# A DiT layer on one Trainium2 core: block-wise storage, one-piece streams and 64-byte gaps for the first feed-forward block's activations

## The reference

```python
mx = split(silu(c) @ ada_w + ada_b, 9)           # shift, scale, gate, three times; mc the same from c_ctx
x = x + 0.5 * mx[2] * swiglu(modulate(rmsnorm(x, norm_ffn1), mx[0], mx[1]), ffn1_w1, ffn1_w3, ffn1_w2)
y = y + 0.5 * mc[2] * swiglu(modulate(rmsnorm(y, norm_ffn1), mc[0], mc[1]), ffn1_w1, ffn1_w3, ffn1_w2)
...
# context keys and states, HGRN2 and Hyena groups of x, w_out
...
x = x + 0.5 * mx[8] * swiglu(modulate(rmsnorm(x, norm_ffn2), mx[6], mx[7]), ffn2_w1, ffn2_w3, ffn2_w2)
return rmsnorm(x, final_norm)
```

## Time and profile before

| | us |
|---|---|
| median of 3 runs | 3288.76 |
| the runs | 3288.66, 3288.76, 3296.98 |
| the profiled execution, its own time | 3298.05 |
| its span, first to last instruction | 3294.4 |
| TensorE busy in the span | 3176.7 (96%) |
| first feed-forward block, first to last matmul | about 228 to 1720 |
| second feed-forward block | about 2520 to 3280 |

### The profile page before, as it was taken

The page is one execution under the profiler, slowest core; times in us unless marked ns, Lnnn a source line. Parts: engine busy times, 40 slices in busy tenths (PEclk is TensorE's granted clock), DMA queues, the critical chain, the costliest instruction groups (busy, mean ns, idle before and its releaser), DMA issues.

```text
span 3294.4 us, 49838 instructions
## 1 busy us (share of the span) xinstructions
PE 3176.7 (96%) x19388; PEld 2796.4 (85%) x19388; DVE 2035.0 (62%) x2657; ACT 1183.0 (36%) x1538; POOL 132.5 (4%) x173
## 2 busy tenths in 40 slices
PE   6979999999999999999988899999998999999998
PEld 2338888888888888888878899999998999999998
DVE  5558747558465675665456567776666555555556
ACT  3122121222222222222236677763334443344434
POOL 1000000000000000000000013430000000000000
PEclk8989999999999999999998999999999999999999
DMA  7647544535446676665323454546544665655563
GB/s 255 224 168 209 168 148 147 179 128 177 150 130 217 204 248 219 220 201 167 99 83 117 139 162 150 154 134 199 165 143 148 183 185 181 184 180 183 179 184 128
DMA packets 438914, 563.28 MB, mean 171 GB/s; under 512 B 17855, under 2 KB 395064, under 8 KB 437896
## 3 DMA queue, kind: packets, MB, share of 16 engines
q1 hardware_dynamic: 432208, 545.80, 52.7%
q0 software_dynamic: 2816, 9.43, 0.9%
q10 hardware_dynamic: 3768, 6.37, 0.6%
HBM read 553.14 MB, written 8.39 MB: 170 GB/s over the span
## 4 chain that ended last, share of the span: by engine, by line
PE 89%; DVE 5%; ACT 2%; issue 2%; DMA 1%; SPq 0%; ACTq 0%; DVEq 0%
PE bank L415 27%; PE bank L416 27%; PE bank L417 27%; PE bank L1070 2%; PE bank L1123 1%; PE bank L649 1%; ACT w_hi L400 1%; PE bank L1311 1%; PE bank L1322 1%; DVE xn L471 1%; PE bank L1230 1%; DMA ada_over<-in_ada_w_dram 1%; DVE csum L958 1%; DVE w_lo L405 1%; PE bank L1111 1%
## 5 line engine op out<-in xcount | busy, mean ns | idle before, releaser
L405 DVE TENSOR_TENSOR w_lo<-raw,w_hi 128x1024 fp32r<-128x1024 f32 x736 | 911.6, 1241 | 963.1 <-ACT w_hi L400 958.8
L400 ACT ACTIVATE w_hi<-raw 128x1024 fp32r<-128x1024 f32 x736 | 774.7, 1057 | 1434.3 <-PE bank L417 1423.2
L415 PE MATMUL bank<-h_hi,w_hi 128*128 128x512 f32 (+1 forms) x2816 | 953.1, 338 | 23.3 <-DVE h_lo L483 20.0
L417 PE MATMUL bank<-h_hi,w_lo 128*128 128x512 f32 (+1 forms) x2816 | 951.1, 338 | 0.0
L416 PE MATMUL bank<-h_lo,w_hi 128*128 128x512 f32 (+1 forms) x2816 | 951.1, 338 | 0.0
L415 PEld LDWEIGHTS bank<-h_hi,w_hi 128*128 128x128 f32 x2816 | 538.2, 191 | 80.5 <-issue 15.8
L416 PEld LDWEIGHTS bank<-h_lo,w_hi 128*128 128x128 f32 x2816 | 538.3, 191 | 55.4
L417 PEld LDWEIGHTS bank<-h_hi,w_lo 128*128 128x128 f32 x2816 | 537.9, 191 | 55.7
L415 PE MATMUL bank<-g_hi,w_hi 128*128 128x512 f32 (+1 forms) x1408 | 476.1, 338 | 5.4 <-DVE g_lo L789 4.7
L416 PE MATMUL bank<-g_lo,w_hi 128*128 128x512 f32 (+1 forms) x1408 | 475.2, 337 | 0.0
L417 PE MATMUL bank<-g_hi,w_lo 128*128 128x512 f32 (+1 forms) x1408 | 474.9, 337 | 0.0
(11 more groups left out here) (244 smaller groups left out, 2796.0 us busy)
## 6 DMA issues: line engine op xcount, KB each, us to landing
raw<-in_ffn_w_dram SPq DMA_DIRECT2D x528, 512.0 KB, 3.6
ada_raw<-in_ada_w_dram SPq DMA_DIRECT2D x260, 512.0 KB, 4.5
raw<-in_w_in_dram SPq DMA_DIRECT2D x176, 512.0 KB, 3.8
raw<-in_w_out_dram SPq DMA_DIRECT2D x32, 512.0 KB, 3.6
ada_over<-in_ada_w_dram SPq DMA_DIRECT2D x28, 512.0 KB, 4.6
spec<-spec_spill POOLq DMA_DIRECT2D x8, 768.0 KB, 5.1
spec_spill<-spec_out ACTq DMA_DIRECT2D x4, 1280.0 KB, 5.1
xin<-in_x_dram SPq DMA_DIRECT2D x1, 2048.0 KB, 9.2
```

The lines of the kernel that those rows point to most:

```text
L400: nc.scalar.activation(w_hi[un.slot(j)][:], raw[un.slot(j)][:], ACT.Copy).then_inc(hi_done, 1)
L405: nc.vector.tensor_tensor(w_lo[un.slot(j)][:], raw[un.slot(j)][:], w_hi[un.slot(j)][:].bitcast(F32), ALU.subtract).then_inc(lo_done, 1)
L415: nc.tensor.matmul(o, w_hi[slot][:, c0:c0 + P], hi, start=start, stop=False, skip_group_check=True)
L417: return nc.tensor.matmul(o, w_lo[slot][:, c0:c0 + P], hi, start=False, stop=stop, skip_group_check=True)
```

## The change

`h1_hi` and `h1_lo` become 16 tiles each, one for each block `kb`, `[P, 2, SEQ]`: the 256 latent and the 256 context columns of a block lie side by side, 2 KB in one piece. The matmul's moving pattern becomes (512 at a step of 1). Behind each of the 32 tiles lies a tile of 16 numbers (64 bytes) that nothing reads or writes, so the tiles start 2112 bytes apart, at offsets 128, 192, 256, ... past a multiple of 1024. The gaps take 2048 bytes of a partition. The same amount is freed by declaring `rows` in the scope `first`, which closes before the feed-forward tiles are declared; `rows` now lies between `window` and `fw1`, and its room is part of the room of the `h1` tiles. All tiles from `cols` to `window`, and those of the later stages, lie 2048 bytes lower; `raw`, `w_hi`, `w_lo`, `x_res`, `g1_hi` and `g1_lo` lie where they were. No instruction is added, removed or moved on any engine, and no wait is added: matmuls, activations and vector operations have the same order, the same sizes and the same counters. Only addresses and that one access pattern differ.

```diff
--- before.py
+++ after.py
@@ -33,6 +33,7 @@
 N_CHUNK = FF // CHUNK
 N_MOD = 9
 EPS = 1e-6
+GAP = 16
 HEADS = 8
 PAIRS = HEADS // 2
 DK = 128
@@ -173,7 +174,6 @@
         ones_d = sb("ones_d", [P, P])
         ones_h = sb("ones_h", [P, P])
         ones_1 = sb("ones_1", [P, P])
-        rows = [sb(f"rows{n}", [P, P]) for n in range(4)]
         cols = [sb(f"cols{n}", [P, P]) for n in range(4)]
         mods = sb("mods", [P, N_MOD, KB, 2])
         silu_c = sb("silu_c", [P, KB, 2])
@@ -206,6 +206,7 @@
         dft = sb("dft", [P, T_COLS], scope=first)
         emb = sb("emb", [FILT_EMB, SEQ], scope=first)
         window = sb("window", [P, TB, HY], scope=first)
+        rows = [sb(f"rows{n}", [P, P], scope=first) for n in range(4)]
         fw1 = sb("fw1", [FILT_EMB, FILT_ORDER], scope=first)
         fw23 = sb("fw23", [FILT_ORDER, 2, FILT_ORDER], scope=first)
         fbias = sb("fbias", [FILT_ORDER, 4], scope=first)
@@ -229,8 +230,15 @@
         ada_wide = ada_raw + ada_over
         first.close()
         ffn = ExitStack()
-        h1_hi = sb("h1_hi", [P, 2, KB, SEQ], F32R, scope=ffn)
-        h1_lo = sb("h1_lo", [P, 2, KB, SEQ], F32R, scope=ffn)
+        h1_hi, h1_lo = [], []
+        for kb in range(KB):
+            letter = "abcdefghijklmnop"[kb]
+            h1_hi.append(sb(f"h1_hi_{letter}", [P, 2, SEQ], F32R, scope=ffn))
+            sb(f"h1_hi_gap_{letter}", [P, GAP], scope=ffn)
+        for kb in range(KB):
+            letter = "abcdefghijklmnop"[kb]
+            h1_lo.append(sb(f"h1_lo_{letter}", [P, 2, SEQ], F32R, scope=ffn))
+            sb(f"h1_lo_gap_{letter}", [P, GAP], scope=ffn)
         g1_hi = [sb(f"g1_hi{b}", [P, 512], F32R, scope=ffn) for b in range(FBLK)]
         g1_lo = [sb(f"g1_lo{b}", [P, 512], F32R, scope=ffn) for b in range(FBLK)]
         ffn.close()
@@ -499,7 +507,7 @@
 
             return vectors[:, bass.ds(kb, 1), t:t + 1].rearrange("p a c -> p (a c)")
 
-        n1["hi_ap"] = lambda t, kb: h1_hi[:, t, kb, :]
+        n1["hi_ap"] = lambda t, kb: h1_hi[kb][:, t, :]
         nctx["hi_ap"] = lambda t, kb: hc_hi[:, kb, :]
         n2["hi_ap"] = lambda t, kb: h2_hi[:, kb, :]
 
@@ -1160,7 +1168,7 @@
             to_columns(ADA_BEFORE - 1)
 
             pe.wait_ge(fs_out, 20)
-            ffn_pe(pe, fa, U_FFN1, lambda k: h1_hi[:, :, k, :], lambda k: h1_lo[:, :, k, :], g1_hi, g1_lo, 512, F1_LOOPS,
+            ffn_pe(pe, fa, U_FFN1, lambda k: h1_hi[k][:], lambda k: h1_lo[k][:], g1_hi, g1_lo, 512, F1_LOOPS,
                    n1["lo"])
 
             norm_pe(pe, nctx, 512)
@@ -1787,10 +1795,10 @@
             ve.wait_ge(mod_done, 3)
             ve.wait_ge(fs_spec, 20)
             ve.wait_ge(fs_dma, 32 * 4)
-            modulate_dve(ve, n1, 0, [x_res, y_res], lambda t, kb: h1_lo[:, t, kb, :], (0, 1), 0, 2, 0, 8)
+            modulate_dve(ve, n1, 0, [x_res, y_res], lambda t, kb: h1_lo[kb][:, t, :], (0, 1), 0, 2, 0, 8)
             take(ADA_BEFORE - 1)
             ve.wait_ge(mod_done, 6)
-            modulate_dve(ve, n1, 0, [x_res, y_res], lambda t, kb: h1_lo[:, t, kb, :], (0, 1), 0, 2, 8, KB)
+            modulate_dve(ve, n1, 0, [x_res, y_res], lambda t, kb: h1_lo[kb][:, t, :], (0, 1), 0, 2, 8, KB)
             ffn_dve(ve, fa, U_FFN1, g1, g1_hi, g1_lo, 512, [x_res, y_res], 0, F1_LOOPS, nctx)
 
             ve.wait_ge(ada_out, 1 + 2 * N_MOD)
```

## The result

| | before | after |
|---|---|---|
| median | 3291.80 us (6 runs, 3288.66 to 3296.98) | 3314.89 us (6 runs, 3312.88 to 3318.94) |
| ratio | | 1.0068, 95% interval 1.0058 to 1.0078 |
| profiled execution | 3298.05 us | 3312.88 us |

What follows compares the result with a forecast made beforehand. TensorE, busy 96% of the span, was taken as the bound. All terms were 0, so 3298.05 us stayed 3298; the forecast was the median level, 3288.8 us, ranging from 6 us under the lowest runs to 3299 us.

Steps and rivals of the forecast that it cites:

- What bounds the kernel: Whole kernel: TensorE busy for 96% of the span, so a change counts by matmul distance or what TensorE waits for.
- One piece in place of two: 4224 matmuls over `h`, first feed-forward block: reading 512 columns in one run instead of two changes nothing, 0 us.
- Gaps of 64 bytes: The 32 `h` tiles start at offsets stepping by 64 bytes: taken as 0; far end 13.4 ns more per matmul.
- The nearest rows: Prologue float32 matmuls of 512 columns, starting at offsets 128 and 960: both median 592 ns, read as no offset cost.
- the 2.3 ns at which the prediction said it would fail: Distance of two starts over `h`, forecast 226.6 ns: the forecast fails if it moves by more than 2.3 ns.
- an odd offset costs something: Slower rival, matmuls over `h`: 30 of 32 tiles cost 13.4 ns more per matmul, 53 us, to 3342 us; chance 4%.
- The rival in which the common offset makes up the fixed part: Faster rival, matmuls over `h`: two runs or shared offset cause the 13.4 ns; up to 56.6 us less, 3232 us; 5%.
- the fixed part: 13.4 ns before each `fp32r` matmul whatever its size, worked out from 226.6 ns at 512 columns and 120.0 at 256.
- The writes, the row tiles, the 2048 bytes: ScalarE and VectorE writes of `h` halves, `rows` freed with the prologue, other tiles moved by 2048 bytes: 0 each.
- Low-clock stretches: Slower rival, pauses between loops of the first feed-forward block: more stretches of 1.6 to 3.2 us; 3299 to 3302; 3%.
- the five stretches of the earlier trace: First feed-forward block, profiled execution: five short stretches at granted clock 0.54 to 0.72, said to cost 11.2 us.
- the two levels: Times of whole runs: the median's level, 3288.8 us, and an upper level, about 3297 to 3298 us.

Runs made afterwards that it cites:

- the kernel with the row tiles alone: The kernel before with only the row tiles freed with the prologue and an unused 2048-byte tile behind `h1_lo`: 3293.12 us, ratio 1.0000.

## Why the prediction was wrong, step by step

- **What bounds the kernel.** Right: TensorE's distance of starts set the time, and nearly all of the change lies in it.
- **One piece in place of two: 0.** Right. One piece without gaps gave 226.7 ns and a ratio of 0.9989; the rule of the Trainium skill that was weighed there ("Advanced Engine Details and Errata", section "PSUM Cachelines") did not show for the moving operand; its section is on PSUM, and neither kernel changes the pattern that the matmuls write.
- **Gaps of 64 bytes: 0.** Wrong, and this is the step that failed. The nearest rows, plain float32 matmuls at offsets of 128 and 960, follow each other only every 428 ns or so, and their durations were taken as proof for a stream of half that distance. The prediction named that weakness and took the value anyway. The rows also compared absolute offsets, which the kernel with everything 64 bytes further showed to play no part. What counts is the distance to the weights, and the prediction did not read these rows for it: by the order of the declarations `dft`, the weights of `tsum` and `tdif`, starts where `h1_hi` does, so those two stood 64 bytes past their weights all along, and at their slow pace no cost showed. The prediction also had no row of an `fp32r` stream at another offset, and treated that absence as a small matter; the absence was the whole question, for the kernel before had every such stream at the offset of its weights. The measured price is 5.1 ns x 4224 = 21.5 us, 226.8 to 231.9 ns, over twice the 2.3 ns at which the prediction said it would fail.
- **The rival "an odd offset costs something"** had the right mechanism and sign with a chance of 4%. Its size was off in both factors: 13.4 ns for 30 tiles of 32 were 53 us; in fact it was 5.1 ns over all 32. In 256 bytes, the measure that counts, eight tiles and not two kept their offset, and these lose about 3 ns too, through the after-effect.
- **The rival in which the common offset makes up the fixed part** found nothing at 512 columns: no offset was under 226.8 ns. At 256 columns it was half right, with 113 to 120 ns in place of 120 and up to 6.7 of the 13.4 ns gone; the changed kernel touches none of these.
- **The writes, the row tiles, the 2048 bytes: 0.** Right, by the 478 to 483 ns of the modulation and by the kernel with the row tiles alone.
- **Low-clock stretches.** The profiled execution before was 9.3 us above the median of its three runs, which the prediction put down to the five stretches of the earlier trace rows. That was less than half of it. A sixth stretch, 1675 to 1686 us at a clock of 0.84, was left out; with it they cost 13 us by the prediction's own sum. The kernel with the row tiles alone has four as well in an execution of 3289.26 us, for 8.5 us. Between these two executions, 8.8 us apart, the first block differs by 3.9 us (1506.5 against 1725.1 - 222.5 = 1502.6) and the prologue by 5.5 us (228.0 against 222.5). The changed kernel's execution has seven, one of them in a new place (704 to 710 us), for 17 us, and a prologue 7.8 us shorter. So executions of either level have such stretches, their places and number change, and in these pairs the prologue scattered more than they did. That the 11.2 us of the sum came near the distance of the two levels was luck. The range rested on these levels and on no bound of the offset; with the far end of that cost in it, as the text had worked it out, it would have reached 3342 us.

## What to carry to other kernels

Where weights are swapped at every matmul, place the moving tiles by their address relative to the weight tiles, modulo 256 bytes, and measure the distance of starts for each stream width: here 512 columns wanted offset 0, and 256 columns gained at most other offsets, most with a whole stage at 192 (113 to 118 ns). For the 512-column stream padding in multiples of 256 bytes was free, and any other cost 2 to 7 ns for each matmul. And when all rows of a trace share one property, they say nothing on what happens without it; a change that breaks such a property deserves a wide range on its other side.

## What the runs showed of the hardware

- The time from one `fp32r` matmul to the next depends on where its moving operand starts relative to the weights in 256 bytes: 226.8 ns at 0, 228.9 at 64, 232 to 234 elsewhere at 512 columns; 120.0 ns at 0 and 113 to 120 elsewhere at 256 columns. Moving everything together by 64 bytes changes nothing (226.7 ns). Why the two addresses matter is not shown.
- A run of 2 KB and two runs of 1 KB, 2 or 16 KB apart, stream at the same pace (226.7 ns, 227 ns and 226.7 ns).
- An offset has an after-effect of about six matmuls on the tile behind it (226, 236, 228, 232, 231, 227 ns at offset 0 behind offset 192, then 227).
- With 256 columns at offset 192, one program ran nearly a whole stage at 113.2 ns in one execution and at 117.7 ns in another, at the same granted clock; the executions lie 23.8 us apart.
